# Four of sixteen weight remainders of a feed-forward stage made by ScalarE and an adding DMA in place of VectorE

## The chip, the core and the metric

The kernel runs on one core of one Trainium2 chip. The metric is the time of one execution on the device in microseconds (us). Its engines are TensorE (PE, matmul; PEld is its weight load), VectorE (DVE), ScalarE (ACT), GpSimd (POOL) and SyncE (SP). SP and POOL issue DMAs here; 16 DMA engines carry them.

## What is computed

Two transformer blocks over 256 tokens of width 2048, in float32. The first has a state-space mixer beside sparse attention, then a gated feed-forward stage; the second has two other mixers and a feed-forward stage with a convolution. The change is in the first block's gate and up projections:

```python
D_FF = -((-8 * D_MODEL) // (3 * 256)) * 256        # 5632
    v = rmsnorm(h, ffn_norm_w[l])
    h = h + (jax.nn.silu(v @ w_gate[l]) * (v @ w_up[l])) @ w_down[l]
```

## The kernel before, in words

Every weight matrix is streamed once from HBM. A float32 weight `w` is split into `hi`, the value rounded to the type `fp32r` in which the matmuls take it, and the remainder (the "rest") `lo = w - hi`. The activations are split likewise. Three products are summed in PSUM: x_hi by w_hi, x_hi by w_lo, x_lo by w_hi (lines 2396 to 2398).

The unit of this stream is a **step**: 256 rows of weights (`SK` = 2 tiles of 128) by `CW` = 512 columns, 512 KB. Step n uses slot n % 4 of three rings in SBUF: `raw` (as loaded), `whi` and `wlo`. For each step:

- SP waits until the rest of step n - 4 is made (`lo_ready`), since that frees the raw slot, and issues the load (line 495; the count that it waits for is in `chunk`, line 505). SP's queue is in order.
- ACT waits for the load (`raw_landed`) and until TensorE is done with step n - 4 (`step_used`), and writes `whi` as a rounded copy (`split`, line 706).
- DVE waits for that (`hi_ready`) and writes `wlo = raw - whi` (line 1462), which counts up `lo_ready`.
- PE waits for `lo_ready`, does 12 matmuls of 128x512 (2 tiles of rows, 2 tiles of tokens, 3 products) and counts up `step_used`.

The stage "ffn1" computes the gate and up projections. 5632 columns are `NFF` = 11 pieces of 512, and each piece is a **pair**: 8 steps of `w_gate`, then 8 steps of `w_up`, numbered 0 to 15 within the pair below. Its steps are 128 to 303 of the stream, so step k of a pair uses slot k % 4. The first pair is written out and the other ten are a hardware loop on ACT, DVE and PE. Between steps 3 and 4 of a pair PE transposes the product of the pair before (`f1_turn`, line 2874, eight transposes into PSUM); ACT and DVE split that product too (lines 1078 and 1960). ACT and DVE walk through the steps four ahead of PE: in each quarter of a pair a hook runs first (ACT: the split of the product behind split 7, the silu of the gate, line 1089, behind split 11), then four splits.

On POOL there is nothing in this stage: its program is a list of small loads and side work, and each waits for its semaphore in order.

The change and the prediction touch `chunk` on SP, `split` and `pair` in `ffn` on ACT and DVE, POOL's program, and the waits of PE in `step`, `last_steps`, `f1_pair` and `f2_chunk`.

Of the kernel before, what the change touches and what calls it, by code (L numbers as in the profile page):

```python
# [69 lines left out]
RING = 4  # L70
NFF = FF // CW


# [104 lines left out]
def two_blocks(nc, a, upto=99):  # L178
# [5 lines left out]
    with ctx:  # L184
# [175 lines left out]
        def sem(name):  # L360
            return ctx.enter_context(nc.semaphore(name))


        raw_landed = [sem(f"raw_landed{i}") for i in range(RING)]
        hi_ready, lo_ready, step_used = sem("hi_ready"), sem("lo_ready"), sem("step_used")
        chunk_out = [sem("chunk_out0"), sem("chunk_out1")]
# [22 lines left out]
        zeroed = sem("zeroed")  # L389
        hid_turned, k_rot = sem("hid_turned"), sem("k_rot")  # L390
        cmp_sum, cmp_kv = sem("cmp_sum"), sem("cmp_kv")

        cv_turned, cv_first, cv_sum, cv_act = sem("cv_turned"), sem("cv_first"), sem("cv_sum"), sem("cv_act")
        xt_turned = sem("xt_turned")
        dt_exp, dt_u, dt_ln, adt_ready = sem("dt_exp"), sem("dt_u"), sem("dt_ln"), sem("adt_ready")
        acum_sum, acum_ready, decay_col = sem("acum_sum"), sem("acum_ready"), sem("decay_col")
        seg_low, seg_sum, seg_exp = sem("seg_low"), sem("seg_sum"), sem("seg_exp")
        cb_sum, cb_masked, m_ready, xs_ready = sem("cb_sum"), sem("cb_masked"), sem("m_ready"), sem("xs_ready")
        yd_sum, st_sum, st_ready, yo_sum, z_silu, ys_ready = (
            sem("yd_sum"), sem("st_sum"), sem("st_ready"), sem("yo_sum"), sem("z_silu"), sem("ys_ready"))  # L400
        xt_out = sem("xt_out")
# [11 lines left out]

        lf_exp, lf_ln, lf_ready = sem("lf_exp"), sem("lf_ln"), sem("lf_ready")
        fq_turned, fq_out, fk_out, fc_sum, fc_out = sem("fq_turned"), sem("fq_out"), sem("fk_out"), sem("fc_sum"), sem("fc_out")
# [16 lines left out]
        tri = C[:, C_TRI:C_TRI + P]  # L432
        tri64 = C[:, C_TRI64:C_TRI64 + P]

        def bank4(n):
# [57 lines left out]
        def _(sp):  # L493
# [10 lines left out]

            def chunk(w, c0, width, j0, j1, s, d):

                for j in range(j0, j1):
                    n = s + j
                    if n >= RING:
                        sp.wait_ge(lo_ready, n - RING + 1 + d)  # L510
                    src = a[w][0, j * SK * P:(j + 1) * SK * P, ds(c0, width)].rearrange("(k p) n -> p k n", p=P)
                    dst = raw[:, n % RING, 0:SK * width].rearrange("p (k n) -> p k n", k=SK)
                    load(dst, src, raw_landed[n % RING])
# [12 lines left out]
            for name, g in G.items():  # L526
                ch, S_, N = g["chunks"], g["S"], g["N"]
                if name in ("ffn1", "ffn2"):
                    (wa, ca, _), (wb, cb, _) = ch[0], ch[1]
                    with sp.Fori(0, NFF) as i:  # L530
                        chunk(wa, i * CW + ca, CW, 0, S_, N, i * (2 * S_))
                        chunk(wb, i * CW + cb, CW, 0, S_, N + S_, i * (2 * S_))
                elif name == "out2":
                    for c, j0, j1, n0 in ((0, 0, 4, 0), (1, 0, 4, 4), (0, 4, 8, 4), (1, 4, 8, 8), (2, 0, 8, 16), (3, 0, 8, 24)):
                        chunk(*ch[c], j0, j1, N + n0, 0)
                elif name == "out1":
                    for c, j0, j1, n0 in ((0, 4, 8, -4), (1, 4, 8, 0), (0, 0, 4, 8), (1, 0, 4, 12), (2, 0, 8, 16), (3, 0, 8, 24)):
                        chunk(*ch[c], j0, j1, N + n0, 0)
                elif name == "in1":
                    chunk(*ch[0], RING, S_, N, 0)  # L540
                    for c in range(1, len(ch)):
                        chunk(*ch[c], 0, S_, N + c * S_, 0)
                elif S_ == FKT // SK:
                    with sp.Fori(0, 2) as i:
                        chunk(ch[0][0], i * (2 * CW), CW, 0, S_, N, i * (2 * S_))
                        chunk(ch[0][0], i * (2 * CW) + CW, CW, 0, S_, N + S_, i * (2 * S_))
                elif S_ % RING == 0 and name != "in2":
                    with sp.Fori(0, len(ch)) as i:
                        chunk(ch[0][0], i * CW, CW, 0, S_, N, i * S_)
                else:  # L550
                    for c in range(len(ch)):
                        chunk(*ch[c], 0, S_, N + c * S_, 0)
# [21 lines left out]
        def _(pool):  # L574
# [56 lines left out]
            if upto >= 2:  # L631
# [30 lines left out]
                load(PIN[:], a["p_2"][0, 0].rearrange("(t p) d -> p t d", p=P), p_landed)  # L662

            if upto >= 10:
                pool.wait_ge(f_lo, NFF)
                load(GP[:], a["final_norm_w"].partition_broadcast(P), gain_landed)

                pool.wait_ge(step_used, G["down1"]["end"])
                pool.memset(HS[:], 0.0).then_inc(zeroed, 1)
                pool.wait_ge(fo_out, 8)  # L670
                load(GP[:], a["g_mix_post_2"][0].partition_broadcast(P), gain_landed)
# [14 lines left out]
        def _(act):  # L686
# [11 lines left out]
            def split(n, d=0, w=None):  # L698

                if n >= NSTEP:  # L700
                    return
                w = SK * (w or WIDTH[n])
                act.wait_ge(raw_landed[n % RING], 16 * (n // RING + 1) + d * (16 // RING))
                if n >= RING:
                    act.wait_ge(step_used, n - RING + 1 + d)
                A(whi[:, n % RING, 0:w], raw[:, n % RING, 0:w], ACT.Copy).then_inc(hi_ready, 1)  # L706

            def stream(g, evac, between={}, loop=True):
# [137 lines left out]
            def dt_log():  # L846
                act.wait_ge(dt_u, 2)
                A(SD[:, 6:8, :], SD[:, 4:6, :], ACT.Ln).then_inc(dt_ln, 1)

# [34 lines left out]
            def hid_out():  # L884
                act.wait_ge(hid_turned, 1)
                hid_k, hid_v = (pt[:, b, 0:P].rearrange("p (m c) -> p m c", c=64) for b in (1, 0))
                A(HK[:], hid_k[:, :, 0:60], ACT.Copy).then_inc(hid_act, 1)
                act.wait_ge(zeroed, 2)
                for m in range(2):
                    for h in range(NKV):  # L890
                        x = hid_v[:, m, h * NCMP:(h + 1) * NCMP].unsqueeze(1).to_broadcast([P, 4, NCMP])
                        ins = A(HV[:, m, h, :, 0:NCMP], x, ACT.Copy)
                ins.then_inc(hid_act, 1)
# [152 lines left out]
            def ffn(g, hooks, between):  # L1046
# [4 lines left out]
                def pair(c, d, between={}):  # L1051
                    for h in range(4):
                        hooks[h](c, d)
                        for j in range(4):
                            between.get(4 * h + j, no)()
                            split(N + c * 16 + 4 * (h + 1) + j, d * 16, CW)

# [83 lines left out]
            def fox_log():  # L1141

                act.wait_ge(lf_ready, 1)
                A(SF_[:, 16:32], SF_[:, 16:32], ACT.Exp, scale=-1.0).then_inc(lf_exp, 1)
                act.wait_ge(lf_exp, 1)
                A(SF_[:, 16:32], SF_[:, 16:32], ACT.Ln, bias=1.0).then_inc(lf_ln, 1)
# [297 lines left out]
        def _(dve):  # L1444
# [203 lines left out]
            def dt_rest():  # L1648
                dve.wait_ge(dt_ln, 1)

# [75 lines left out]
            def y_off():  # L1726

                dve.wait_ge(yo_sum, 1)
                link(V.tensor_tensor(hd(YOFF[:]), pt[:, 2:4, :].rearrange("p b (h d) -> p (b h) d", d=HD),
# [187 lines left out]
            def ffn(g, hooks, between):  # L1917
                N = g["N"]

                def pair(c, d, between={}):  # L1920
                    for h in range(4):
                        hooks[h](c, d)
                        for j in range(4):
                            between.get(4 * h + j, no)()
                            split(N + c * 16 + 4 * (h + 1) + j, d * 16, CW)

# [446 lines left out]
        def _(pe):  # L2373
# [9 lines left out]
            def step(n, d, b, kt0, w, first, last, hi=AH, lo=AL):  # L2383

                if n:
                    pe.wait_ge(lo_ready, n + 1 + d)
                for k in range(SK):
# [33 lines left out]
            def last_steps(n, m, b, kt0, hi, lo):  # L2421

                for t in range(NT):
                    o = pg[:, b + t, :]
                    for i in range(m):
                        if t == 0:
                            pe.wait_ge(lo_ready, n + i + 1)
                        for k in range(SK):
# [159 lines left out]
            def hid_turn():  # L2588
                pe.wait_ge(hid_act, 1)
                for i in range(4):  # L2590
                    r = slice(64 * (i // 2), 64 * (i // 2) + 60)
                    ins = tr(pt[:, 1 - i // 2, (i % 2) * 64:(i % 2) * 64 + 60], HT_[r, (i % 2) * P:(i % 2 + 1) * P], C[r, r])
                ins.then_inc(hid_turned, 1)

# [184 lines left out]
            def y_off():  # L2779

                pe.wait_ge(st_ready, 1)
                for g in range(SSD_G):
                    ins = mm(pt[:, 2 + g, :], XC[:, 10 + g, P:TOK], STA[:, g, :], start=True, stop=True)
                ins.then_inc(yo_sum, 1)

# [91 lines left out]
            def f1_pair(c, d):  # L2877
                dc, dn = d * 2, d * 16
                if c:
                    chunk(F1, 2 * c, 0, 4, dc, dn)  # L2880
                    f1_turn(c, d)
                    chunk(F1, 2 * c, 4, 8, dc, dn)
                else:
                    chunk(F1, 0, before=last_quarter(G["out1"], 2))
                chunk(F1, 2 * c + 1, dc=dc, dn=dn)

# [11 lines left out]
            def f2_chunk(c, m, d, j0=0, j1=8, before=no):  # L2898
# [3 lines left out]
                for j in range(j0, j1):  # L2902
# [3 lines left out]
                    n = F2["N"] + 16 * c + 8 * m + j  # L2906
                    pe.wait_ge(lo_ready, n + 1 + d * 16)
                    for k in range(SK):
# [292 lines left out]
            def proj(c, hi, lo, between=no):  # L3201

                n = proj_step(c)
                pe.wait_ge(p_lo, 1 + c // 2)
                pe.wait_ge(lo_ready, n + 1)
                for k in range(SK):
# [150 lines left out]
```

## Time and profile before

| | |
|---|---|
| Median of 2 runs | 2429.11 us (2428.98 and 2429.25) |
| Span of the profiled execution, first to last instruction | 2426.9 us |
| Granted TensorE clock, mean | 1.000 |
| PE busy | 2418.2 us (100%) |
| DVE busy | 1484.9 us (61%) |
| ACT busy | 1262.1 us (52%) |
| POOL busy | 47.2 us (2%) |
| DMA moved | 448.51 MB, mean 185 GB/s |

The profile names a group of instructions by its line, engine, operation and tiles (output <- inputs). "Idle before" is the time for which the engine stood still just ahead of an instruction, with the one that released it. For the profiled execution only the span is recorded, not a time with what lies around it; the span is 2.2 us below the median of the runs. Matmul ends are modelled and matmuls overlap, so TensorE's pace is read from the spacing of starts, and its waits from the list of waits.

### The profile page before, as it was taken

To read this page: it belongs to the slowest core of one execution; us is meant where nothing else is said; L and a number is where in the kernel's file an instruction comes from. 1 tells how busy PE (TensorE), PEld (TensorE's weight loads), DVE (VectorE), ACT (ScalarE), POOL (GpSimd) and SP (SyncE) were. 2 spreads that over 40 slices of the span, in tenths; PEclk is the share of its full clock that TensorE was granted. 3 is DMA by queue.
4 is the path that set the end of the run, shared out by engine and by line. 5 is a ranking of instruction groups with operands and counts; after the bars stand their busy time and mean duration, and the time that the engine had idled before them with its cause. 6 is when DMAs were issued, how large, how long until landed. Compare 5 with 4: busy or idle time off the path is not lost.

```text
span 2426.9 us, 35530 instructions
## 1 busy us (share of the span) xinstructions
PE 2418.2 (100%) x13377; PEld 2044.9 (84%) x13377; DVE 1484.9 (61%) x1814; ACT 1262.1 (52%) x1598; POOL 47.2 (2%) x105
## 2 busy tenths in 40 slices
PE   9999999999999999999999999999999999999999
PEld 8888888888888888888888888898888888888887
DVE  6478765454454454444568665567777777644465
ACT  5467754444444444444655445466566656444464
POOL 2300000000000000000000000000000000000000
PEclk9999999999999999999999999999999999999999
DMA  8644546666666666556565555666565655665654
GB/s 270 190 140 117 152 167 185 191 190 186 189 190 188 190 191 206 190 190 190 164 192 171 166 149 181 191 191 190 189 191 174 203 185 189 203 203 193 210 194 152
DMA packets 235098, 448.51 MB, mean 185 GB/s; under 512 B 14368, under 2 KB 31604, under 8 KB 234480
## 3 DMA queue, kind: packets, MB, share of 16 engines
q1 hardware_dynamic: 231712, 434.83, 58.3%
q0 software_dynamic: 3280, 12.21, 1.6%
q8 instruction: 73, 1.20, 0.2%
q14 instruction: 33, 0.27, 0.0%
HBM read 443.84 MB, written 3.15 MB: 184 GB/s over the span
## 4 chain that ended last, share of the span: by engine, by line
PE 98%; ACT 1%; DVE 0%; DMA 0%; issue 0%; SPq 0%; ACTq 0%; DVEq 0%
PE pg L2396 21%; PE pg L2398 21%; PE pg L2397 21%; PE pt L2892 7%; PE pg L2892 6%; PE pg L2896 3%; PE pt L2896 3%; PE pg L2455 3%; PE pg L2456 3%; PE pg L2457 3%; PE pt L2467 1%; PE pt L2651 1%; PE pt L2680 0%; PE pt L2667 0%; PE pt L2874 0%; PE pg L2894 0%
## 5 line engine op out<-in xcount | busy, mean ns | idle before, releaser
L1462 DVE TENSOR_TENSOR wlo<-raw,whi 128x1024 fp32r<-128x1024 f32 (+3 forms) x843 | 1002.5, 1197 | 873.0 <-ACT whi L706 871.8
L706 ACT ACTIVATE whi<-raw 128x1024 fp32r<-128x1024 f32 (+3 forms) x843 | 870.6, 1036 | 1097.4 <-PE pg L2398 810.7
L2396 PE MATMUL pg<-whi,A 128*128 128x512 f32 (+1 forms) x1216 | 470.7, 387 | 0.0
L2398 PE MATMUL pg<-whi,A 128*128 128x512 f32 (+1 forms) x1216 | 466.7, 384 | 0.0
L2397 PE MATMUL pg<-wlo,A 128*128 128x512 f32 (+1 forms) x1216 | 466.3, 383 | 0.0
L2396 PE MATMUL pg<-whi,FH 128*128 128x512 f32 x696 | 271.2, 390 | 0.0
L2398 PE MATMUL pg<-whi,FL 128*128 128x512 f32 x696 | 270.8, 389 | 0.0
L2397 PE MATMUL pg<-wlo,FH 128*128 128x512 f32 x696 | 270.8, 389 | 0.0
L2398 PEld LDWEIGHTS pg<-whi,A 128*128 128x128 f32 x1216 | 228.3, 188 | 45.3
L2396 PEld LDWEIGHTS pg<-whi,A 128*128 128x128 f32 x1216 | 228.3, 188 | 44.4 <-DVE A L1601 0.4
L2397 PEld LDWEIGHTS pg<-wlo,A 128*128 128x128 f32 x1216 | 228.5, 188 | 43.7
L2892 PE MATMUL pt<-A,whi 128*128 128x512 f32 x704 | 244.8, 391 | 0.0
L2892 PE MATMUL pg<-A,whi 128*128 128x512 f32 x640 | 222.3, 391 | 0.0
L2896 PE MATMUL pg<-A,wlo 128*128 128x256 f32 x704 | 197.3, 280 | 0.0
L2896 PE MATMUL pt<-A,wlo 128*128 128x256 f32 x704 | 197.1, 280 | 0.0
L2892 PEld LDWEIGHTS pt<-A,whi 128*128 128x128 f32 x704 | 131.7, 187 | 28.9
L2397 PEld LDWEIGHTS pg<-wlo,FH 128*128 128x128 f32 x696 | 130.7, 188 | 27.1
L2398 PEld LDWEIGHTS pg<-whi,FL 128*128 128x128 f32 x696 | 130.6, 188 | 27.1
L2396 PEld LDWEIGHTS pg<-whi,FH 128*128 128x128 f32 x696 | 130.7, 188 | 27.0
L2892 PEld LDWEIGHTS pg<-A,whi 128*128 128x128 f32 x640 | 119.7, 187 | 26.2
L2896 PEld LDWEIGHTS pg<-A,wlo 128*128 128x128 f32 x704 | 133.2, 189 | 0.0
L2896 PEld LDWEIGHTS pt<-A,wlo 128*128 128x128 f32 x704 | 133.1, 189 | 0.0
(539 smaller groups left out, 2706.4 us busy)
## 6 DMA issues: line engine op xcount, KB each, us to landing
raw<-w_up SPq DMA_DIRECT2D x264, 512.0 KB, 3.8
raw<-w_down SPq DMA_DIRECT2D x176, 512.0 KB, 4.3
raw<-w_in SPq DMA_DIRECT2D x151, 512.0 KB, 3.7
raw<-w_gate SPq DMA_DIRECT2D x88, 512.0 KB, 3.6
raw<-w_out SPq DMA_DIRECT2D x64, 512.0 KB, 3.7
raw<-w_ple_gate SPq DMA_DIRECT2D x32, 512.0 KB, 4.5
raw<-w_in SPq DMA_DIRECT2D x32, 388.0 KB, 3.3
raw<-w_in SPq DMA_DIRECT2D x16, 280.0 KB, 3.1
```

Of the source, the lines that this page charges most:

```text
L706: A(whi[:, n % RING, 0:w], raw[:, n % RING, 0:w], ACT.Copy).then_inc(hi_ready, 1)
L1462: V.tensor_tensor(wlo[:, n % RING, 0:w], raw[:, n % RING, 0:w], whi[:, n % RING, 0:w].bitcast(F32), ALU.subtract).then_inc(lo_ready, 1)
L2396: mm(o, xh, wh, start=first and k == 0, stop=False)
L2397: mm(o, xh, wl, start=False, stop=False)
L2398: ins = mm(o, xl, wh, start=False, stop=last and k == SK - 1)
L2455: mm(o, xh, wh, start=j == 0 and k == 0, stop=False)
L2456: mm(o, xh, wl, start=False, stop=False)
L2457: ins = mm(o, xl, wh, start=False, stop=j == 7 and k == SK - 1)
L2467: ins = tr(pt[:, g % 4, (2 * k + t) * P:(2 * k + t + 1) * P], src(2 * g + k, t), ident)
L2651: ins = mm(pt[:, e, c0:c0 + nk], QT[pr, 2 * kv + x, t * P:(t + 1) * P], KTT[pr, b, kv, 0:nk], start=True, stop=True)
L2892: mm(o.rearrange("p (a n) -> p a n", a=2), wh, A2[:, :, kt, :], start=first, stop=False)
L2896: return mm(o[:, 0:TOK], wl, AH[:, kt, :], start=False, stop=last)
```

## The change

For steps 5, 7, 9 and 11 of each of the eleven pairs (44 of 176 steps), DVE no longer makes the rest. ACT writes `wlo = -round(raw)` with a second activation of scale -1, then `whi = round(raw)` as before; POOL waits for `hi_ready` and issues a DMA from `raw` to `wlo`, both in SBUF, that adds what it carries to what stands there: `wlo = raw - round(raw)`. PE waits for that DMA (`added[0..3]`, one semaphore for each of the four places) before such a step, and SP waits for it before it loads raw slot anew. `lo_ready` counts only the rests that DVE makes, so every wait on it goes through `los(n)`, which subtracts the added ones up to n. SP's loop over the pairs is unrolled. A few semaphores of other stages are merged to make room for the four new ones, with the same order of work.

The core of the diff:

```diff
+ADDED = (5, 7, 9, 11)
...
+        added = [sem(f"added{i}") for i in range(len(ADDED))]
...
+        def los(n):
+
+            q = n - G["ffn1"]["N"]
+            return n + 1 - sum(16 * i + k <= q for i in range(NFF) for k in ADDED)
...
-            def chunk(w, c0, width, j0, j1, s, d):
+            def chunk(w, c0, width, j0, j1, s, d, pair=None):
...
-                        sp.wait_ge(lo_ready, n - RING + 1 + d)
+                        sp.wait_ge(lo_ready, los(n - RING + d) if isinstance(d, int) else los(n - RING) + d)
+                    if pair is not None and n - RING - G["ffn1"]["N"] in ADDED:
+                        sp.wait_ge(added[ADDED.index(n - RING - G["ffn1"]["N"])], pair * 16 + 16)
...
+                if name == "ffn1":
+                    for i in range(NFF):
+                        chunk(*ch[2 * i], 0, S_, N, i * (2 * S_))
+                        chunk(*ch[2 * i + 1], 0, S_, N + S_, i * (2 * S_), i)
...
+            def add_raw(i):
+                for k, q in enumerate(ADDED):
+                    n = (G["ffn1"]["N"] + q) % RING
+                    pool.wait_ge(hi_ready, G["ffn1"]["N"] + q + 1 + i * 16)
+                    pool.dma_start(wlo[:, n, :].bitcast(F32), raw[:, n, :], accum_op=ALU.add).then_inc(added[k], 16)
...
+            def split_added(n, d):
+
+                act.wait_ge(raw_landed[n % RING], 16 * (n // RING + 1) + d * (16 // RING))
+                act.wait_ge(step_used, n - RING + 1 + d)
+                A(wlo[:, n % RING, :], raw[:, n % RING, :], ACT.Copy, scale=-1.0)
+                A(whi[:, n % RING, :], raw[:, n % RING, :], ACT.Copy).then_inc(hi_ready, 1)
...
-                            split(N + c * 16 + 4 * (h + 1) + j, d * 16, CW)
+                            if g is G["ffn1"] and 4 * (h + 1) + j in ADDED:
+                                split_added(N + c * 16 + 4 * (h + 1) + j, d * 16)
+                            else:
+                                split(N + c * 16 + 4 * (h + 1) + j, d * 16, CW)
...
+                            if g is G["ffn1"] and 4 * (h + 1) + j in ADDED:
+                                continue
                             split(N + c * 16 + 4 * (h + 1) + j, d * 16, CW)
...
-                    pe.wait_ge(lo_ready, n + 1 + d)
+                    pe.wait_ge(lo_ready, los(n) + d)
...
-                dc, dn = d * 2, d * 16
+                dc, dn = d * 2, d * (16 - len(ADDED))
+
+                def rests(m, also=no):
+
+                    def before(j):
+                        also(j)
+                        if 8 * m + j in ADDED:
+                            pe.wait_ge(added[ADDED.index(8 * m + j)], 16 * (c + 1) + d * 16)
+                    return before
...
-                chunk(F1, 2 * c + 1, dc=dc, dn=dn)
+                chunk(F1, 2 * c + 1, dc=dc, dn=dn, before=rests(1))
```

How the rows of the program stand, at three places. The first is ScalarE in the loop over pairs 1 to 10, from the head of the loop to the split of the product (L1078 before, L1111 now), which covers the splits of steps 4 to 7. Before:

```order
L706 ACTIVATE whi<-raw 128x1024 [waits step_used]
L705 REGISTER_ALU [waits raw_landed1]
L706 ACTIVATE whi<-raw 128x1024 [waits step_used]
L705 REGISTER_ALU [waits raw_landed2]
L706 ACTIVATE whi<-raw 128x1024 [waits step_used]
L705 REGISTER_ALU [waits raw_landed3]
L706 ACTIVATE whi<-raw 128x1024 [waits step_used]
L1077 REGISTER_ALU
L1078 ISA [waits f_turned]
L1078 ACTIVATE FH<-pt 128x1024
```

Now:

```order
L729 ACTIVATE whi<-raw 128x1024 [waits step_used]
L734 REGISTER_ALU [waits raw_landed1]
L735 ACTIVATE wlo<-raw 128x1024 [waits step_used]
L736 ACTIVATE whi<-raw 128x1024
L728 REGISTER_ALU [waits raw_landed2]
L729 ACTIVATE whi<-raw 128x1024 [waits step_used]
L734 REGISTER_ALU [waits raw_landed3]
L735 ACTIVATE wlo<-raw 128x1024 [waits step_used]
L736 ACTIVATE whi<-raw 128x1024
L1110 REGISTER_ALU
L1111 ISA [waits f_turned]
L1111 ACTIVATE FH<-pt 128x1024
```

Steps 5 and 7 have two activations each, and the rounded copy that POOL and the later engines wait for is the second of them.

The second place is SP, the loads of one pair as the program now has them (before, each load waits on `lo_ready` alone). The first row is the gate half, the others are the up half, steps 8 to 15:

```order
L502 DMA raw<-w_gate 128x2x512 [waits lo_ready] x8
L502 DMA raw<-w_up 128x2x512 [waits lo_ready]
L502 DMA raw<-w_up 128x2x512 [waits added0,lo_ready]
L502 DMA raw<-w_up 128x2x512 [waits lo_ready]
L502 DMA raw<-w_up 128x2x512 [waits added1,lo_ready]
L502 DMA raw<-w_up 128x2x512 [waits lo_ready]
L502 DMA raw<-w_up 128x2x512 [waits added2,lo_ready]
```

The load for step 9 waits for the DMA of step 5, 11 for 7, 13 for 9 and 15 for 11, and each has the load for the next even step behind it in the queue.

The third is POOL's program around the new DMAs:

```order
L589 DMA PIN<-p 128x2x256 [waits step_used]
L681 DMA wlo<-raw 128x1024 [waits hi_ready] x44
L589 DMA GP<-final_norm_w 128x2048 [waits f_lo]
```

The 44 DMAs stand where nothing stood before, each behind its own wait.

## Rows read from the trace of the kernel before

**Rows 1.** The page: span, and each engine's busy time, share of the span and instructions.

```profile
span 2426.9 us, 35530 instructions
PE 2418.2 (100%) x13377; PEld 2044.9 (84%) x13377; DVE 1484.9 (61%) x1814; ACT 1262.1 (52%) x1598; POOL 47.2 (2%) x105
```

**Rows 2.** Table of windows, ten pairs of the stage; the first row names the columns.

```profile
core 0: us, PE busy (x) PEld busy (x) DVE busy (x) ACT busy (x) POOL busy (x), PEclk, DMA share, GB/s
464.70:909.00 444.30, 444.30 (x2001) 368.71 (x2000) 220.63 (x191) 190.68 (x190) 0.00 (x0) 1.00 0.65 189
```

**Rows 3.** All waits in 464.7 to 909.0 us: total, times, longest.

```profile
ACT whi L706 <- PE pg L2398: 253.6, 160, 1.7
DVE wlo L1462 <- ACT whi L706: 225.2, 161, 1.5
```

**Rows 4.** Timeline: start, duration, engine, instruction, idle before and its releaser.

```profile
595.55 1.03 PE L2874 MATMUL pt<-C,HT 128*128 128x128 f32 x8
596.34 0.48 PE L2396 MATMUL pg<-whi,A 128*128 128x512 f32 x1
...
602.07 1.06 ACT L706 ACTIVATE whi<-raw 128x1024 fp32r<-128x1024 f32 x1 [1.66 <-PE pg L2398]
604.79 1.06 ACT L706 ACTIVATE whi<-raw 128x1024 fp32r<-128x1024 f32 x1 [1.66 <-PE pg L2398]
607.51 1.06 ACT L706 ACTIVATE whi<-raw 128x1024 fp32r<-128x1024 f32 x1 [1.66 <-PE pg L2398]
610.23 1.06 ACT L706 ACTIVATE whi<-raw 128x1024 fp32r<-128x1024 f32 x1 [0.51 <-PE pg L2398]
```

**Rows 5.** Tile FL, VectorE's row: ns min/median/max, first and last start.

```profile
L1960 DVE TENSOR_TENSOR FL<-pt,FH x11: 1216/1217/1218, 464.7 to 909.0; 128x1024 f32 x10, 128x1024 fp32r<-128x1024 f32 x1
```

**Rows 6.** Groups by line, 464.7 to 909.0 us: busy, mean ns, idle before.

```profile
L1462 DVE TENSOR_TENSOR wlo<-raw,whi 128x1024 fp32r<-128x1024 f32 x161 | 197.4, 1226 | 225.2 <-ACT whi L706 225.2
L706 ACT ACTIVATE whi<-raw 128x1024 fp32r<-128x1024 f32 x160 | 169.7, 1061 | 253.6 <-PE pg L2398 253.6
L1089 ACT ACTIVATE SG<-pg,SM 128x512 f32<-128x512 f32 x20 | 12.5, 674 | 0.0
```

**Rows 7.** SP's waits, 464.7 to 909.0 us.

```profile
SPq L495 <- DVE wlo L1462: 351.1, 160, 3.1
```

**Rows 8.** Timeline of POOL, 184 to 912 us (all of its rows there).

```profile
184.37 0.73 POOL L576 DMA_DIRECT2D PIN<-p  x1 [68.66 <-PE pg L2457]
910.55 0.55 POOL L576 DMA_DIRECT2D GP<-final_norm_w  x1 [725.45 <-DVE FL L1960]
```

**Rows 9.** Tile W1K: POOL's four loads of 512 KB, ns to issue, us to landing.

```profile
L576 POOL DMA_DIRECT2D W1K<-cmp_w_k x4: 748/754/789, 44.5 to 58.2; - x4
...
DMA to landing us min/median/max: 4.1/5.1/6.2
```

**Rows 10.** DMA view, 464.7 to 909.0 us: packets, MB, share; issues, KB, us to landing.

```profile
q1 hardware_dynamic: 43519, 83.89, 65.0%
...
raw<-w_up SPq DMA_DIRECT2D x77, 512.0 KB, 3.6
raw<-w_gate SPq DMA_DIRECT2D x72, 512.0 KB, 3.6
raw<-w_down SPq DMA_DIRECT2D x11, 512.0 KB, 3.7
```

**Rows 11.** The page, DMA queues: POOL's.

```profile
q0 software_dynamic: 3280, 12.21, 1.6%
```

**Rows 12.** Tile E: POOL's two transfers of 1024 KB, us to landing.

```profile
DMA to landing us min/median/max: 6.8/7.7/8.6
```

**Rows 13.** DMA view, 595.5 to 604 us in 40 slices: busy tenths.

```profile
DMA  6000987559998520099349999930000000999479
```

More of the change, by code:

```diff
@@ L389, in two_blocks @@
         zeroed = sem("zeroed")
-        hid_turned, k_rot = sem("hid_turned"), sem("k_rot")
+        k_rot = sem("k_rot")
         cmp_sum, cmp_kv = sem("cmp_sum"), sem("cmp_kv")
@@ L394, in two_blocks @@
         xt_turned = sem("xt_turned")
-        dt_exp, dt_u, dt_ln, adt_ready = sem("dt_exp"), sem("dt_u"), sem("dt_ln"), sem("adt_ready")
+        dt_exp, dt_u, adt_ready = sem("dt_exp"), sem("dt_u"), sem("adt_ready")
         acum_sum, acum_ready, decay_col = sem("acum_sum"), sem("acum_ready"), sem("decay_col")
@@ L398, in two_blocks @@
         cb_sum, cb_masked, m_ready, xs_ready = sem("cb_sum"), sem("cb_masked"), sem("m_ready"), sem("xs_ready")
-        yd_sum, st_sum, st_ready, yo_sum, z_silu, ys_ready = (
-            sem("yd_sum"), sem("st_sum"), sem("st_ready"), sem("yo_sum"), sem("z_silu"), sem("ys_ready"))
+        yd_sum, st_sum, st_ready, z_silu, ys_ready = (
+            sem("yd_sum"), sem("st_sum"), sem("st_ready"), sem("z_silu"), sem("ys_ready"))
         xt_out = sem("xt_out")
@@ L412, in two_blocks @@
             sem("c_first"), sem("c_part"), sem("c_sum"), sem("c_silu"), sem("c_prod"))
-        lf_exp, lf_ln, lf_ready = sem("lf_exp"), sem("lf_ln"), sem("lf_ready")
+        lf_ln, lf_ready = sem("lf_ln"), sem("lf_ready")
         fq_turned, fq_out, fk_out, fc_sum, fc_out = sem("fq_turned"), sem("fq_out"), sem("fk_out"), sem("fc_sum"), sem("fc_out")
@@ L527, in _ @@
                 ch, S_, N = g["chunks"], g["S"], g["N"]
-                if name in ("ffn1", "ffn2"):
+                if name == "ffn1":
+                    for i in range(NFF):
+                        chunk(*ch[2 * i], 0, S_, N, i * (2 * S_))
+                        chunk(*ch[2 * i + 1], 0, S_, N + S_, i * (2 * S_), i)
+                elif name == "ffn2":
                     (wa, ca, _), (wb, cb, _) = ch[0], ch[1]
@@ L662, in _ @@
                 load(PIN[:], a["p_2"][0, 0].rearrange("(t p) d -> p t d", p=P), p_landed)
+            def add_raw(i):
[3 more added lines that the diff above has]
+                    pool.dma_start(wlo[:, n, :].bitcast(F32), raw[:, n, :], accum_op=ALU.add).then_inc(added[k], 16)
+            if upto >= 9:
+                for i in range(NFF):
+                    add_raw(i)
             if upto >= 10:
@@ L847, in dt_log @@
                 act.wait_ge(dt_u, 2)
-                A(SD[:, 6:8, :], SD[:, 4:6, :], ACT.Ln).then_inc(dt_ln, 1)
+                A(SD[:, 6:8, :], SD[:, 4:6, :], ACT.Ln).then_inc(dt_exp, 1)
             def decays():
@@ L884, in hid_out @@
             def hid_out():
-                act.wait_ge(hid_turned, 1)
+                act.wait_ge(hid_sum, 2)
                 hid_k, hid_v = (pt[:, b, 0:P].rearrange("p (m c) -> p m c", c=64) for b in (1, 0))
@@ L1143, in fox_log @@
                 act.wait_ge(lf_ready, 1)
-                A(SF_[:, 16:32], SF_[:, 16:32], ACT.Exp, scale=-1.0).then_inc(lf_exp, 1)
-                act.wait_ge(lf_exp, 1)
+                link(A(SF_[:, 16:32], SF_[:, 16:32], ACT.Exp, scale=-1.0))
                 A(SF_[:, 16:32], SF_[:, 16:32], ACT.Ln, bias=1.0).then_inc(lf_ln, 1)
@@ L1648, in dt_rest @@
             def dt_rest():
-                dve.wait_ge(dt_ln, 1)
+                dve.wait_ge(dt_exp, 3)
                 link(V.tensor_scalar(dt2(4), dt2(8), 0.0, None, ALU.is_equal))
@@ L1726, in y_off @@
             def y_off():
-                dve.wait_ge(yo_sum, 1)
+                dve.wait_ge(st_sum, 2)
                 link(V.tensor_tensor(hd(YOFF[:]), pt[:, 2:4, :].rearrange("p b (h d) -> p (b h) d", d=HD),
@@ L2426, in last_steps @@
                         if t == 0:
-                            pe.wait_ge(lo_ready, n + i + 1)
+                            pe.wait_ge(lo_ready, los(n + i))
                         for k in range(SK):
@@ L2592, in hid_turn @@
                     ins = tr(pt[:, 1 - i // 2, (i % 2) * 64:(i % 2) * 64 + 60], HT_[r, (i % 2) * P:(i % 2 + 1) * P], C[r, r])
-                ins.then_inc(hid_turned, 1)
+                ins.then_inc(hid_sum, 1)
             def cmp():
@@ L2783, in y_off @@
                     ins = mm(pt[:, 2 + g, :], XC[:, 10 + g, P:TOK], STA[:, g, :], start=True, stop=True)
-                ins.then_inc(yo_sum, 1)
+                ins.then_inc(st_sum, 1)
             def ssd_tiles(k, t):
@@ L2877, in f1_pair @@
             def f1_pair(c, d):
-                dc, dn = d * 2, d * 16
+                dc, dn = d * 2, d * (16 - len(ADDED))
[5 more added lines that the diff above has]
+                    return before
                 if c:
-                    chunk(F1, 2 * c, 0, 4, dc, dn)
+                    chunk(F1, 2 * c, 0, 4, dc, dn, before=rests(0))
                     f1_turn(c, d)
-                    chunk(F1, 2 * c, 4, 8, dc, dn)
+                    chunk(F1, 2 * c, 4, 8, dc, dn, before=rests(0))
                 else:
-                    chunk(F1, 0, before=last_quarter(G["out1"], 2))
-                chunk(F1, 2 * c + 1, dc=dc, dn=dn)
+                    chunk(F1, 0, before=rests(0, last_quarter(G["out1"], 2)))
+                chunk(F1, 2 * c + 1, dc=dc, dn=dn, before=rests(1))
             def f2_step(n, d, k, i, o, both, first, last):
@@ L2906, in f2_chunk @@
                     n = F2["N"] + 16 * c + 8 * m + j
-                    pe.wait_ge(lo_ready, n + 1 + d * 16)
+                    pe.wait_ge(lo_ready, los(n) + d * 16)
                     for k in range(SK):
@@ L3204, in proj @@
                 pe.wait_ge(p_lo, 1 + c // 2)
-                pe.wait_ge(lo_ready, n + 1)
+                pe.wait_ge(lo_ready, los(n))
                 for k in range(SK):
```

## The prediction

> **What bounds the kernel now.** The page comes first: TensorE is busy for 2418.2 of 2426.9 us, with VectorE at 61% and ScalarE at 52% [rows 1]. A full engine can still be full of waits that the records hide, so the second view is the table of windows over the stretch of the change, ten of its eleven pairs: TensorE is busy for 444.30 of 444.30 us at a granted clock of 1.00 [rows 2]. The third is the list of waits in that stretch. It holds only ScalarE waiting for TensorE (160 times) and VectorE waiting for ScalarE (161 times), and TensorE doesn't stand in it [rows 3]. So the chain is TensorE's own work, and VectorE's 220.63 us there [rows 2] set nothing. Fourth, the timeline gives the beat: ScalarE starts a split every 2.72 us, each released by TensorE [rows 4]; that is one step of 12 matmuls. (A silu between two splits only shortens one wait.) From one FL row to the next there are (909.0 - 464.7)/10 = 44.43 us [rows 5], which is 16 steps of 2.72 (43.52) and 0.91 for the eight transposes behind step 3 [rows 4]; the steps of a pair are numbered 0 to 15 here. None of this gets shorter by what the change does. **It can gain nothing from TensorE and can only lose by making it wait.**
>
> **The change part by part.** VectorE loses 4 x 11 = 44 subtractions of 1.226 us [rows 6], 54 us, all off the path: worth 0. ScalarE gains 44 copies; the trace has none with a scale, so I take the plain copy of the same shape, 1.061 us [rows 6], 47 us (between that and 1.35, twice the 674 ns of a 128x512 activation [rows 6]). With 190.68 of 444.30 us busy [rows 2] it has room, but in an added step the whole sequence gets longer. The unrolled SP loop issues the same 176 loads, SP waits 351.1 us of this stretch anyway [rows 7]: 0. The merged semaphores elsewhere carry the same order of work: 0. POOL stands idle from 184.37 to 910.55 us, and behind the 44 issues comes only a gain load that waits for the last pair anyway [rows 8]: 0.
>
> What decides is when the rest of an added step is there. All that follows is the estimate of one pair, in us from the end of its step 1 (which frees slot 1). Without stalls step 3 ends at 5.4, step 5 starts at 9.1 (three steps and the transposes) and ends at 11.8, step 7 starts at 14.5 and ends at 17.2, step 9 starts at 20.0, step 11 at 25.4.
>
> The prices. ScalarE: 0.1 after the slot is free, two copies 2.1, 0.1 to the issue: the DMA is issued 2.3 after. A DMA from POOL of the same 512 KB took 4.1 us at best and 5.1 in the median, issue to landing [rows 9]. Its engine time: the loads of this stretch hold all 16 engines for 65.0% of 444.3 us, for 77 + 72 + 11 = 160 loads [rows 10]: 1.8 us each; POOL's queue holds them for 1.6% of 2426.9 us for 12.21 MB [rows 11], 1.7 us for 512 KB. So POOL's DMA costs about 2.3 beyond its engine time (4.1 - 1.8; I put 1.6 before its data and 0.7 behind), and a load 1.8 beyond (3.6 - 1.8; 1.1 and 0.7) [rows 10]. **The unknown term** is the engine time of an accumulating DMA; no trace of before has one. Below: 1.8, if the second read is free. Above: 3.6, if both operands pass at the cost of a plain transfer; transfers of 1024 KB from POOL took 6.8 to 8.6 us [rows 12], where 2.3 + 3.6 = 5.9 is the quiet case. Source and target lie in SBUF, which may shorten the reads, and the second read may overlap the write: I take the middle, 2.7.
>
> With 2.7, where transfers that overlap share the engines evenly:
> - Step 5: issued 2.3, landed 2.3 + 2.3 + 2.7 = 7.3, wanted 9.1. No stall. But SP's loads for steps 9 and 10 now leave together at 7.3: step 9 needs raw slot 1, which the DMA was reading, and step 10 is queued behind it. Their data starts at 8.4.
> - Step 7: slot free 5.4, issued 7.7, data from 9.3. By then 2.7 of the loads is left; 2.7 beside 2.7 ends at 14.7, landed 15.4, wanted 14.5. **Stall 0.9.**
> - Step 9: its raw lands at 11.8, just in time. Issued 14.1, data from 15.7; the loads for 11 and 12 leave at 15.4, data from 16.5; 1.9 left, shared, ends 20.3, landed 21.0, wanted 20.0 + 0.9. **Stall 0.1 to 0.2.**
> - Step 11: its raw lands at 20.8, where step 7 ended at 18.1: 2.7 late. Issued 23.0, data from 24.6, beside what is left of loads 13 and 14 (1.1): landed 29.1, wanted 25.4 + 1.1. **Stall 2.6.** The nine steps up to the next added one are split as before and catch up.
>
> Together 3.7 us a pair, 41 us for eleven. The stage ends 41 us later, and all behind it hangs on TensorE, so nothing gives it back: 2426.9 + 41 = 2468. The median of the runs, 2429.11, lies 2.2 above the span, so the time is **2470 us**, 1.7% more. About 2% (48.6 us, 4.4 a pair) is what a measurement of this kernel tells from no change.
>
> The only traffic in [rows 10] is plain loads, one read for one write. The Trainium skill, "Collectives: The Full Stack", The bandwidth ceiling: the fold count and why AG ≠ RS ≠ AR, states that an adding transfer is slow not by the addition but because it needs two source reads through one ring, and so runs at half the copy rate. By that rule the engine time would be the upper end, 3.6, and the sum that of the second rival below; no run here shows it yet.
>
> **The rivals.**
> 1. *It keeps up: not slower.* If the second read is nearly free (1.8), step 7 lands at 13.6 before 14.5 and step 9 at 20.0 in time; step 11's raw is 0.8 late and it lands 0.7 late. 11 x 0.7 = 8 us: 2437, and 2429 if the fixed part is half a microsecond less. For it: between the bursts of two loads the engines stand idle for 1 to 1.5 us (slices of 0.21 us that read 0) [rows 13], and 35% of their time is unused [rows 10]. Against it: the stall of step 11 hangs on raw slots, not on idle engines. It decides from an engine time below about 2. Chance 0.25.
> 2. *Two full reads: slower.* With 3.6: step 7 lands at 16.3 (stall 1.8), step 9 at 21.9 (0.1 to 0.2), step 11 at 30.9, wanted 27.4 (3.5). 5.5 a pair, 60 us: 2490. It passes 2% from about 3.1. For it: 6.8 to 8.6 us for twice the bytes [rows 12]. Chance 0.17.
> 3. *The adder is slower than the reads.* With 6 us of engine time step 5 itself lands 1.5 late, steps 7, 9 and 11 lose 4.2, 4.4 and 4.2 because each DMA also waits for the one before and for the loads it let pile up: 14.3 a pair, 158 us: 2587. No row speaks for it, and none excludes it. Chance 0.11.
> 4. *VectorE's relief helps.* It would need TensorE to wait for VectorE somewhere, and [rows 3] has no such wait; or a matmul beat that depends on VectorE, while the beat of 2.72 is the same through all [rows 4]. Chance 0.02.
>
> **How the numbers follow.** The forecast case (0.45) has engine times from 2 to 3.3 and gives 2440 to 2485. Two thirds of it lie within 2%, with all of rival 1: 0.30 + 0.25 = 0.55. Slower: 0.15 + 0.17 + 0.11 = 0.43. Faster: 0.02. The range begins at 2427, the time before less its spread, since rival 1 holds a quarter, and ends at 2535, between rivals 2 and 3, which leaves out most of rival 3 and rival 4. The likeliest case's own range is 2440 to 2485.
>
> **What would show it.** In the profile after: TensorE with waits for the DMA into wlo, most in total before steps 11 and 7 of a pair and none before step 5; the FL rows some 48 us apart in place of 44.43; VectorE 54 us less busy, ScalarE 47 more; loads for odd steps of the second half of a pair issued only when an added rest has landed, in twos; 5.0 us and more from issue to landing of the new DMA; outside this stage nothing moved. I am wrong if the new DMA lands within 4.5 us (rival 1), if step 5 stalls (rival 3, or a fixed part that is far above 2.3), or if TensorE's beat of 2.72 changes.

## The result and the profile after

The changed kernel takes 2463.66 us (2463.09 and 2464.23) against 2429.11: the ratio is 1.0141, interval 1.0124 to 1.0158. That is 34.6 us slower, where 41 were forecast. It is within the 2% that was taken as no change, yet the interval lies clear of 1, so the kernel did get slower.

The page of the changed kernel: span, then each engine's busy time and share, and POOL's DMA queue (packets, MB, share of 16 engines).

```profile
span 2461.2 us, 35127 instructions
...
PE 2428.8 (99%) x13377; PEld 2045.7 (83%) x13377; DVE 1429.8 (58%) x1770; ACT 1300.6 (53%) x1642; POOL 85.0 (3%) x149
...
q0 software_dynamic: 9616, 35.28, 6.8%
```

Against [rows 1], VectorE is 55 us less busy and ScalarE 38 more (47 were expected). TensorE has the same 13377 matmuls.

All waits in the stage's ten loop pairs, 467.9 to 943.1 us (total, times, longest):

```profile
POOL wlo L681 <- ACT whi L736: 416.6, 39, 27.0
DVE wlo L1494 <- ACT whi L729: 269.0, 103, 8.6
ACT whi L729 <- PE pg L2432: 112.7, 86, 5.6
ACT wlo L735 <- DMA raw<-w_up: 54.6, 10, 5.7
ACT wlo L735 <- PE pg L2432: 48.1, 29, 1.7
ACT whi L729 <- DMA raw<-w_up: 36.1, 8, 5.0
DVE FL L1994 <- ACT FH L1111: 34.9, 10, 3.5
PEld pg L2430 <- DMA wlo<-raw: 31.2, 22, 2.5
PE pg L2430 <- DMA wlo<-raw: 22.4, 20, 2.1
```

In [rows 3] TensorE did not stand in this list at all. Now its matmuls and weight loads wait for the adding DMA, about two times a pair, and ScalarE waits for raw weights, which it never did. The PE and PEld rows tell of the same waits and must not be added: a weight load runs ahead of its matmul, so its record starts to wait sooner.

The FL row (VectorE; min/median/max ns, first and last start):

```profile
L1994 DVE TENSOR_TENSOR FL<-pt,FH x11: 1218/1224/1226, 467.9 to 943.1; 128x1024 f32 x10, 128x1024 fp32r<-128x1024 f32 x1
```

Ten pairs now take 943.1 - 467.9 = 475.2 us, 47.52 each in place of 44.43 [rows 5]: 30.9 us. The first pair adds 467.9 - 464.7 = 3.2. That is 34.1 of the 34.3 us by which the span grew (2461.2 - 2426.9); nothing before or behind the stage moved by more than the rest of it.

One pair in the timeline: ScalarE's copies and POOL's issues for steps 5, 7, 9 and 11 (start, duration, instruction, idle before and its releaser).

```profile
602.97 1.06 ACT L735 ACTIVATE wlo<-raw 128x1024 fp32r<-128x1024 f32 x1 [1.66 <-PE pg L2432]
605.27 0.86 POOL L681 DMA_DIRECT2D wlo<-raw  x1 [27.02 <-ACT whi L736]
608.41 1.06 ACT L735 ACTIVATE wlo<-raw 128x1024 fp32r<-128x1024 f32 x1 [1.66 <-PE pg L2432]
610.72 0.86 POOL L681 DMA_DIRECT2D wlo<-raw  x1 [4.59 <-ACT whi L736]
614.74 1.06 ACT L735 ACTIVATE wlo<-raw 128x1024 fp32r<-128x1024 f32 x1 [1.65 <-PE pg L2432]
617.04 0.86 POOL L681 DMA_DIRECT2D wlo<-raw  x1 [5.47 <-ACT whi L736]
617.78 0.50 PE L2430 MATMUL pg<-whi,A 128*128 128x512 f32 x1 [0.36 <-DMA wlo<-raw]
623.98 1.06 ACT L735 ACTIVATE wlo<-raw 128x1024 fp32r<-128x1024 f32 x1 [5.46 <-DMA raw<-w_up]
626.28 0.86 POOL L681 DMA_DIRECT2D wlo<-raw  x1 [8.38 <-ACT whi L736]
630.71 0.50 PE L2430 MATMUL pg<-whi,A 128*128 128x512 f32 x1 [1.75 <-DMA wlo<-raw]
```

The chain of waits through the same pair (start, duration, what):

```profile
609.38 1.05 ACT whi L736
610.43 0.28 issue
610.72 7.03 DMA wlo<-raw
617.80 6.08 DMA raw<-w_up
624.26 0.68 issue
624.95 1.05 ACT whi L736
626.00 0.28 issue
626.28 4.38 DMA wlo<-raw
630.71 0.50 PE pg L2430
```

Read together: step 5's slot is free at 602.9 and its DMA goes off 2.3 later, as reckoned. Step 7's DMA needs 7.03 us and TensorE waits for it at 617.78. Its landing releases the load of step 11, which takes 6.08 us beside step 9's DMA; so ScalarE starts step 11 at 623.98, where TensorE had freed the slot at 620.5 (617.78 + 2.72). Step 9 is in time. Step 11's DMA then runs alone and takes 4.38, but it started 3.4 us late, and TensorE waits again. Outside the stage the chain of this kernel is TensorE's work as before.

### The profile page after: what moved, and what is told of

Its sections match the earlier page's. It is cut to its first block, busy times and chain, and to the rows that moved or that the text cites. A ratio compares the mean times of both kernels' runs of the same rounds, so it can differ in the third digit from the quotient of the medians.

```text
span 2461.2 us, 35127 instructions
## 1 busy us (share of the span) xinstructions
PE 2428.8 (99%) x13377; PEld 2045.7 (83%) x13377; DVE 1429.8 (58%) x1770; ACT 1300.6 (53%) x1642; POOL 85.0 (3%) x149
## 4 chain that ended last, share of the span: by engine, by line
PE 89%; DMA 8%; ACT 2%; issue 1%; DVE 1%; ACTq 0%; SPq 0%; DVEq 0%
PE pg L2430 18%; PE pg L2432 18%; PE pg L2431 18%; PE pt L2935 7%; PE pg L2935 6%; DMA wlo<-raw 5%; PE pg L2939 3%; PE pt L2939 3%; PE pg L2489 3%; DMA raw<-w_up 3%; PE pg L2490 3%; PE pg L2491 3%; ACT whi L736 1%; PE pt L2501 1%; PE pt L2685 1%
## 5 line engine op out<-in xcount | busy, mean ns | idle before, releaser
L1494 DVE TENSOR_TENSOR wlo<-raw,whi 128x1024 fp32r<-128x1024 f32 (+3 forms) x799 | 946.7, 1195 | 922.9 <-ACT whi L729 921.8
L729 ACT ACTIVATE whi<-raw 128x1024 fp32r<-128x1024 f32 (+3 forms) x799 | 821.9, 1034 | 980.5 <-PE pg L2432 653.8
```

The lines of the kernel that those rows point to most:

```text
L1494: V.tensor_tensor(wlo[:, n % RING, 0:w], raw[:, n % RING, 0:w], whi[:, n % RING, 0:w].bitcast(F32), ALU.subtract).then_inc(lo_ready, 1)
```

## The experiments

Theory: an adding DMA holds the DMA engines longer than a copy, and it is late where loads run beside it; the loads that it let go make the next one late. Rivals are stated with each run. Each ratio is against the kernel before, measured beside it; its times there were 2428.6 to 2429.4 us (medians).

**1. No adding.** The DMA copies raw over wlo, which then holds the raw weight in place of the rest.

```diff
-                    pool.dma_start(wlo[:, n, :].bitcast(F32), raw[:, n, :], accum_op=ALU.add).then_inc(added[k], 16)
+                    pool.dma_start(wlo[:, n, :].bitcast(F32), raw[:, n, :]).then_inc(added[k], 16)
```

> The 44 DMAs copy raw to wlo without adding (wlo then holds the raw weight, not the rest); all else as in the change. Theory (the adding DMA holds the engines 2.9 us where a copy of 512 KB holds them 1.7, and that length, beside the loads that leave in twos, is what makes it late): the DMA lands within about 4 us, no waits of TensorE, 2429 to 2432 us. Rival (it is the fixed path over POOL and the raw slot held for it, whatever the DMA does): the waits stay at 2 to 3 us a pair, 2452 to 2463 us.

Measured: 2431.62 us, ratio 1.0008 (0.9998 to 1.0017). The landing of its DMAs (POOL's, us min/median/max):

```profile
DMA to landing us min/median/max: 2.8/4.0/6.3
```

and of the change's:

```profile
DMA to landing us min/median/max: 4.4/5.1/7.6
```

Same path over POOL, same waits, same held raw slots; only the addition is gone, and with it all but 2.5 us of the loss, which the interval doesn't tell from nothing. The engine time is read in the DMA view, 464.7 to 900 us (POOL's queue: packets, MB, share). First this kernel, then the one of run 6, which adds and has as many DMAs in that stretch, 39:

```profile
q0 software_dynamic: 5617, 20.45, 11.5%
```

```profile
q0 software_dynamic: 5616, 20.45, 23.7%
```

The same packets and bytes hold the engines 0.115 x 435.3 / 39 = 1.28 us for a copy and 0.237 x 435.3 / 39 = 2.65 us for an adding DMA. The change itself, in the same stretch, with the row of its loads:

```profile
q1 hardware_dynamic: 39674, 76.49, 54.8%
q0 software_dynamic: 5248, 19.07, 23.9%
```

5248 packets are 36.4 DMAs, so there an adding DMA holds the engines for 2.86 us, a little more than in run 6 (and in run 5, where each stands alone: 11.6% for 19 DMAs, 2.66). The 76.49 MB are 146 loads of 512 KB, 1.6 us each.

**2. ScalarE's copies alone.**

```diff
+                A(wlo[:, n % RING, :], raw[:, n % RING, :], ACT.Copy, scale=-1.0)
                 A(whi[:, n % RING, :], raw[:, n % RING, :], ACT.Copy).then_inc(hi_ready, 1)
```

> The kernel before, with ScalarE's second activation alone: in the same 44 steps it writes wlo = -round(raw) first and whi after it, and VectorE then overwrites wlo with the rest as before. No DMA. Theory (the whole loss is the DMA's lateness; ScalarE's 47 us more and a rounded copy that is 1 us later are hidden): within 3 us of before, 2427 to 2432. Rival (the later rounded copy is on the path): some 1 us in each of the 44 steps, up to 2473.

Measured: 2429.05 us, ratio 0.9999 (0.9990 to 1.0009). The later rounded copy costs nothing by itself.

**3. SP's order exchanged.**

```diff
-                        chunk(*ch[2 * i + 1], 0, S_, N + S_, i * (2 * S_), i)
+                        for j in (0, 2, 1, 4, 3, 6, 5, 7):
+                            chunk(*ch[2 * i + 1], j, j + 1, N + S_, i * (2 * S_), i)
```

> The change, with SP issuing the load for the next even step ahead of the one that waits for an added rest (8, 10, 9, 12, 11, 14, 13, 15). Theory (about half of the loss is that two loads leave together when an added rest lands and then share the engines with the next adding DMA): the wait before step 7 (0.6 to 1.4 us now) goes, the one before step 11 (1.7 to 2.5) shrinks to about 1; 1 to 1.3 us a pair, 2440 to 2445. Rival (the sum of latencies alone, the order of the loads is no matter): 2460 to 2464.

Measured: 2467.39 us, ratio 1.0156 (1.0139 to 1.0173), no better than the change (2463.66, measured at another time). **This part of the theory fell:** that the loss comes from loads that leave together, and could be ordered away. TensorE's waits moved instead: in one pair before steps 7, 9 and 11 its weight loads waited 0.38, 1.59 and 1.56 us.

**4. Steps 5 and 7 only.**

```diff
-ADDED = (5, 7, 9, 11)
+ADDED = (5, 7)
```

> The change with added rests in steps 5 and 7 only. Theory (steps 9 and 11 are late because they inherit the raw slots of 5 and 7; 5 and 7 themselves lose what they lose now): only the wait before step 7 is left, 0.6 to 1.4 us a pair, 2436 to 2443. Rival (each adding DMA costs the same): half of the loss, 2446.

Measured: 2438.31 us, ratio 1.0036 (1.0023 to 1.0049): 9.2 us, 0.84 a pair, every wait before step 7, whose DMA landed 6.7 to 7.5 us after its issue. Two of four rests cost a quarter of the loss.

**5. Steps 5 and 9 only** (`ADDED = (5, 9)`).

> The change with added rests in steps 5 and 9 only, as many as in the run with 5 and 7 (2438.31 us), four steps apart in place of two, and in one raw slot. Theory (a lone adding DMA has landed before the two loads that it releases can slow the next one; the loss comes from the next adding DMA beside them): no wait of TensorE, 2429 to 2432 us. Rival (step 9 inherits the raw slot of 5 and is late for that): some 1 us a pair, about 2440.

Measured: 2429.50 us, ratio 1.0001 (0.9992 to 1.0011). Landing of its 22 DMAs:

```profile
DMA to landing us min/median/max: 4.4/4.4/6.2
```

Alone, an adding DMA lands in 4.4 us. As many DMAs as in run 4, in one slot, four steps apart: nothing is lost.

**6. Every third step.** The positions are 4, 7, 10 and 13, and SP's wait for an added rest is extended to the gate half of the next pair.

```diff
-ADDED = (5, 7, 9, 11)
+ADDED = (4, 7, 10, 13)
...
+                    q = n - RING - G["ffn1"]["N"]
+                    if pair is not None and q % 16 in ADDED and (q >= 0 or pair > 0):
+                        sp.wait_ge(added[ADDED.index(q % 16)], pair * 16 + (16 if q >= 0 else 0))
...
```

> The change with four added rests a pair in steps 4, 7, 10 and 13: as many DMAs (44), three steps apart, each in another slot (SP's waits moved accordingly, to the next pair's loads too). Theory (in steps 5 to 11 the engines are asked for 2.9 + 2 x 1.65 = 6.2 us in every two steps of 5.44, which is more than they have; every third step it is 2.9 + 3 x 1.65 = 7.9 in 8.2): most of the loss goes, 2435 to 2450 us, with small waits before steps 10 and 13. Rival (44 adding DMAs cost what they cost, wherever they stand): 2460 to 2465.

Measured: 2440.55 us, ratio 1.0048 (1.0032 to 1.0065). All 44 DMAs, two thirds of the loss gone; the 11.1 us that are left are waits before steps 10 and 13, mostly 13.

**7. A bystander.** In the same 44 steps ScalarE and POOL do their part on a spare buffer, VectorE makes every rest, and TensorE does not wait for the DMA.

```diff
+        SIDE = at("SIDE", [P, 2, SK * CW], F32, o_b + (2 * FKT - 4) * TOK * 4)
...
-                    pool.dma_start(wlo[:, n, :].bitcast(F32), raw[:, n, :], accum_op=ALU.add).then_inc(added[k], 16)
+                    pool.dma_start(SIDE[:, n // 2, :], raw[:, n, :], accum_op=ALU.add).then_inc(added[k], 16)
...
-                            pe.wait_ge(added[ADDED.index(8 * m + j)], 16 * (c + 1) + d * 16)
...
```

> All rests made by VectorE as before. In the same 44 steps ScalarE also writes -round(raw) to a spare buffer and POOL adds raw to it by the same DMA; SP waits for that DMA before it loads the raw slot anew, but TensorE does not wait for it. Theory (the loss is TensorE's wait for a late rest; the traffic and the raw slot held longer are covered, since a late load of up to about 3 us meets more than 5 us of slack): 2429 to 2434 us. Rival (the traffic or the held raw slot themselves slow the stage): above 2445.

Measured: 2429.37 us, ratio 1.0003 (0.9994 to 1.0013). Landing of its 44 DMAs:

```profile
DMA to landing us min/median/max: 4.4/5.2/7.6
```

They land as late as the change's (4.4, 5.1 and 7.6), and nothing is lost. The traffic, the contention with the loads and the raw slot held longer cost nothing as long as TensorE doesn't wait for the DMA itself.

**8. Steps 9 and 11 only** (`ADDED = (9, 11)`).

> The change with added rests in steps 9 and 11 only. The same pattern as 5 and 7 (2438.31 us), but no transposes lie in the window of three steps before it, so step 11 is wanted 0.9 us sooner after its slot is free. Theory (the wait before step 11 in the change, 1.7 to 2.5, is this plus what it inherits from 5 and 7): 1.1 to 1.7 us a pair, 2442 to 2448 us, all before step 11. Rival (nothing is inherited, position alone decides): the full 2.2 a pair, 2453.

Measured: 2448.74 us, ratio 1.0082 (1.0065 to 1.0099): 19.3 us, 1.76 a pair, all before step 11, and 0.7 us above the upper end of what was expected (2448; 1.7 a pair). It equals 0.84 + 0.91 = 1.75. The pattern of run 4 costs 0.9 more where the transposes, 0.91 us, don't lie in between. Runs 4 and 8 sum to 28.5 us of the 34.6; the other 6 appear only with all four.

**9. Half loads for steps 9 to 12** (the second half of the raw slot keeps old weights).

```diff
+                    if pair is not None and 1 <= j <= 4:
+                        dst, src = dst[:, 0:1], src[:, 0:1]
                     load(dst, src, raw_landed[n % RING])
```

> The change, with the four loads for steps 9 to 12 of each pair cut to their first half (256 KB; the second half of the raw slot keeps old weights). Waits and order are the change's. Theory (adding DMA and full loads together ask for more engine time than the two steps have): with 2.9 + 2 x 0.8 = 4.5 us asked in 5.44, little waiting is left, at most 0.5 us a pair, 2429 to 2436 us. Rival (the fixed part of the DMA's path and the chain through the raw slot): above 2450.

Measured: 2458.07 us, ratio 1.0125 (1.0105 to 1.0144). A miss that by its number spoke for the rival. The timeline of one pair, DMAs of steps 7, 9 and 11:

```profile
603.64 0.86 POOL L683 DMA_DIRECT2D wlo<-raw  x1 [4.59 <-ACT whi L738]
609.97 0.86 POOL L683 DMA_DIRECT2D wlo<-raw  x1 [5.47 <-ACT whi L738]
615.41 0.86 POOL L683 DMA_DIRECT2D wlo<-raw  x1 [4.58 <-ACT whi L738]
623.31 0.50 PE L2432 MATMUL pg<-whi,A 128*128 128x512 f32 x1 [2.09 <-DMA wlo<-raw]
```

The wait before step 7 is gone, and step 11's raw is in time (its DMA is issued 5.44 us after the one before, the beat of two steps). But that DMA takes until 623.3, 7.9 us, because the loads for 13 and 14, which were whole, left just then. My reckoning had overlooked them. Hence run 11. Part of the median is the clock's: its mean was 0.999 in two executions of 2454 us, and 0.997 and 0.995 in two of 2462.

**10. Only steps 9 and 10 exchanged** in SP's order: `for j in (0, 2, 1, 3, 4, 5, 6, 7)`.

> The change, with one exchange in SP's order in each pair: the load for step 10 ahead of the one for step 9; 11 and 12 stay as they were. In the run with all of them exchanged (2467.39 us) the load for step 12 took the place that 10 had left, beside the DMA of step 7. Theory: now that DMA has only the load for 9 beside it, the wait before step 7 (0.8) goes, and the one before 11 stays or shrinks a little; 1.5 to 2.5 us a pair, 2445 to 2457. Rival (the order of loads does nothing, or harm, as in that run): 2463 or more.

Measured: 2470.29 us, ratio 1.0165 (1.0148 to 1.0182). A second miss of the idea of ordering. POOL's four DMAs of one pair, and the two longest of its three waits of TensorE's weight loads, before steps 7 and 9:

```profile
609.88 0.86 POOL L682 DMA_DIRECT2D wlo<-raw  x1 [27.06 <-ACT whi L737]
615.33 0.86 POOL L682 DMA_DIRECT2D wlo<-raw  x1 [4.59 <-ACT whi L737]
622.04 0.86 POOL L682 DMA_DIRECT2D wlo<-raw  x1 [5.85 <-ACT whi L737]
629.29 0.86 POOL L682 DMA_DIRECT2D wlo<-raw  x1 [6.40 <-ACT whi L737]
```

```profile
622.21 0.19 PEld L2431 LDWEIGHTS pg<-whi,A 128*128 128x128 f32 x1 [0.60 <-DMA wlo<-raw]
629.83 0.19 PEld L2431 LDWEIGHTS pg<-whi,A 128*128 128x128 f32 x1 [2.29 <-DMA wlo<-raw]
```

Step 7's DMA still takes 6.9 us, step 9's now 7.8. The likely reading is that the load for 10, once free to leave at once, runs beside step 5's DMA, which had been alone, and that raw 9 comes later for it; this was read from one timeline and not tested by itself. What the two runs show is that no order of the same loads that I tried helps. Part of this run's time is the clock: its four executions had a mean granted clock of 0.996 to 0.997. In the profiled one TensorE ran at 1.2 GHz in four stretches of the stage, the longest behind a wait of 3.41 us (columns as in [rows 2]):

```profile
821.00:826.00 5.00, 4.26 (x10) 3.43 (x11) 1.23 (x1) 1.06 (x1) 0.00 (x0) 0.50 1.02 272
```

Summed over windows of 1 us, the granted clock costs 8.5 us in this stage, against 3.4 in the change and 1.7 in run 3. Without it this order is no better than the change either (2472.8 - 8.5 against 2463.1 - 3.4, by the profiled executions).

**11. Half loads for steps 9 to 14**, the correction of run 9 (`1 <= j <= 6`).

> As the run with half loads for steps 9 to 12 (2458.07 us), with the loads for 13 and 14 halved too. That run left one wait of 2.1 to 3.1 us a pair, before step 11, though that step's raw was on time: its adding DMA was issued just as the loads for 13 and 14 left at full size. Theory (an adding DMA lands in 4.4 us alone and later by the engine time of each load beside it, 1.6 us for a full one): all four now meet at most 1.6 us of loads, 6.0 against 5.8 that are allowed, 0 to 0.5 us a pair, 2429 to 2435 us. Rival (the fixed path and the chain through the raw slots, to which sizes of loads are no matter): as before, 2450 or more.

Measured: 2431.97 us, ratio 1.0012 (1.0003 to 1.0022). With no full load beside the four adding DMAs, 32 of 34.6 us are gone, with every wait, every slot and the number of DMAs as in the change. This excludes the rival of run 9: the fixed path and the held slots are the same here and lose 3 us.

## Why the prediction was right, point by point

**The number.** 34.6 us were lost where 41 were forecast, and 2463.66 lies in the likeliest case's own range, 2440 to 2485. The full range, 2427 to 2535, was so wide that it held the time of before too, so lying in it says little; what bears the prediction out is the place of the waits.

**The bound.** TensorE set the time and nothing could be gained: VectorE lost 55 us of work, and no run is faster than before by more than its interval: neither run 1, with the same 44 subtractions gone and next to no wait, nor run 5. ScalarE's 44 copies hide (run 2); they came to 38 us in place of 47, in part since the second copy of a step starts 0.09 us before the first ends (603.94 against 602.97 + 1.06).

**The unknown term.** 2.7 us was the middle between 1.8 and 3.6. It is 2.65 us in run 6 and 2.86 in the change, beside 1.28 for a plain copy between the same buffers. So an adding DMA takes 2.07 times the copy by run 6's row. The middle was a guess between two bounds, and that it fell so near is luck. The Trainium skill, "Collectives: The Full Stack", The bandwidth ceiling: the fold count and why AG ≠ RS ≠ AR, has an adding transfer run at half the copy rate. By that rule it would be 2 x 1.28 = 2.6: the factor agrees with the trace. That two reads are the cause, no run here shows. What was off was the base: the load's 1.8 is no price for a copy inside SBUF. So the second rival, "two full reads", took the factor of two from a base too high, and its 60 us did not come. By its own terms it should have been more: with 3.6 step 7 lands at 9.3 + 3.6 + 3.6 + 0.7 = 17.2 and not at 16.3.

**The fixed part** was mis-sized: 2.3 was taken, and it is 4.4 - 2.65 = 1.75. The even share of the engines was wrong too, the other way. With 1.75, 2.65 and loads of 1.6 us, the prediction's own sum would have loads and adding DMA end at 7.8 + 3.2 + 2.65 = 13.65, and step 7 land at 14.2 to 14.4, before the 14.5 at which it is wanted: no stall. Measured, its DMA takes 7.0 to 7.6 us, so it lands at 14.7 to 15.3. Overlap costs more than the engine times added up. So the stall of step 7 was forecast in the right place and nearly the right size by errors that cancel, and that is luck. At step 11 two more errors cancel in part: its raw was 3.4 late and not 2.7, while its own DMA landed in 4.4 and not in 6.1, since by then it was alone. And 3.3 us of the measured loss are TensorE's lower clock (last section), which the sum did not have: the waits alone cost about 31 us against the 41.

**The places.** Expected waits before steps 5, 7, 9 and 11 were 0, 0.9, 0.1 to 0.2 and 2.6. The weight loads' records over the eleven pairs give 0, 0.6 to 1.4, 0 to 0.2 and 1.5 to 2.5, in the mean 0, 0.9, 0 and 2.2. Step 5 is never waited for. One of the signs of being wrong was badly chosen: "if the new DMA lands within 4.5 us". A DMA that meets no load does land in 4.4 (step 11's above), and yet the first rival is not what happened; only the median, 5.1, is as forecast.

**The mechanism**, with run numbers: the DMA is issued 2.3 us after the slot is free, and TensorE wants the rest 8.2 us after that moment, or 9.1 where the transposes lie in between. So 5.9 or 6.8 us are left for it. It lands in 4.4 alone (5), in 7.0 to 7.6 beside two loads in the change, and in up to 8.4 (8, 9). Two steps apart, each adding DMA meets the loads that the one before released. One such meeting a pair is enough for a loss (4, 8, 9). All four together ask for 2.65 + 2 x 1.6 = 5.9 us of engine time in every 5.44. The two orders tried don't mend this (3, 10); smaller loads do (11), a copy in place of an addition does (1), and distance does (5, in part 6). That the sum fits the spacing is not enough by itself: run 6 asks for 2.65 + 3 x 1.6 = 7.5 us in every 8.2 and still loses 1.0 a pair. Why overlap costs more than the sum, no run shows.

**The rivals.** "It keeps up" needed an engine time below 2, and 2.65 excludes it; the copy of run 1, at 1.28, is what it would have looked like (2431.62 us, in the 2429 to 2437 that it gave). "The adder is slower than the reads" needed 6 us and a stall of step 5, and neither is there. "VectorE's relief helps" is excluded by runs 1 and 5.

## What to carry to other kernels

Where TensorE sets the time, as here, moving work off VectorE gains nothing, and the new path is judged by its latency against the lead that the ring gives (three steps here), not by its throughput. Price a DMA by a row of the same kind (inside SBUF, adding), with the loads beside it added, and look at what its completion releases: that traffic meets the next one. If such DMAs must be used, space them so that each lands before the loads released by the last one can slow it. With two a pair, four steps apart lost nothing and two steps 9 to 19 us; with four a pair, three steps apart lost 11 us in place of 35. Four a pair at four steps was not tried.

## What was not expected of the hardware

The clock granted to TensorE fell in two of the eleven pairs. TensorE's matmuls, in the timeline of the change:

```profile
579.60 0.39 PE L2432 MATMUL pg<-whi,A 128*128 128x512 f32 x1
582.01 0.80 PE L2430 MATMUL pg<-whi,A 128*128 128x512 f32 x1 [2.02 <-DMA wlo<-raw]
582.60 0.63 PE L2431 MATMUL pg<-wlo,A 128*128 128x512 f32 x1
583.03 0.63 PE L2432 MATMUL pg<-whi,A 128*128 128x512 f32 x1
583.46 0.63 PE L2430 MATMUL pg<-whi,A 128*128 128x512 f32 x1
```

After a wait of 2.02 us the matmuls start 0.43 us apart in place of 0.23, at the lower level of 1.2 GHz (the table of windows, whose columns are those of [rows 2], shows it):

```profile
579.00:582.00 3.00, 0.99 (x5) 0.49 (x3) 2.77 (x3) 2.09 (x3) 0.00 (x0) 1.00 0.78 155
582.00:583.00 1.00, 0.99 (x2) 0.83 (x3) 0.73 (x1) 0.00 (x0) 0.00 (x0) 0.51 0.00 0
583.00:586.00 3.00, 3.00 (x10) 2.37 (x9) 0.00 (x0) 0.00 (x0) 0.00 (x0) 0.59 0.99 296
```

It is back at 2.4 GHz by 585.5. The pairs in which this happened took 1.6 us longer (POOL's first issues of successive pairs lie 47.0 to 47.8 us apart, 47.3 in the mean, and 48.9 and 49.0 in these two), so about 3.3 of the 34.6 us are the clock's. Other pairs had waits as long before the same step (2.05 to 2.09 us in three of them) and kept the clock, and so did run 8 behind one of 2.67 us. Waits of 2 us cost more than themselves only sometimes; what decides it, the runs don't tell.

A load beside an adding DMA took longer too: 6.08 us in the chain above, where 3.6 was the median in [rows 10].
